# The mLSTM's gates made ahead of its queries, keys and values; the first key lists fetched behind the retention

## What is computed

```
# block 1, after attention and retention
x = x + mix @ w_out
q = (rmsnorm(x) @ w_query)                      # routing of PEER
s = einsum('thpd,hpnd->thpn', q, sub_keys)      # sub_keys: the "key lists"
# block 2, token mixer
c_gate, b_gate, x_in, q, k, v, o, i_pre, f_pre, ga, gm = split(h @ w_in)
ya = b_gate * causal_dwconv(c_gate * x_in)
q, k = split(silu(causal_dwconv(concat(q, k))))
logf = log_sigmoid(f_pre + b_fgate);  b = cumsum(logf)
dlog = b[t] - b[s] + i_pre[s];  m_t = max over s <= t
num = sum_s (q.k) * exp(dlog - m_t) * v;  den = sum_s (q.k) * exp(dlog - m_t)
h = num / max(|den|, exp(-m_t))
```

## Time and profile before

| what | us |
|---|---|
| median of 3 runs (3684.33 to 3688.38) | 3687.12 |
| the profiled execution's own time | 3683.72 |
| span of its trace | 3681.7 |

### The profile page before, as it was taken

The page is one execution under the profiler, slowest core; times in us unless marked ns, Lnnn a source line. Parts: engine busy times, 40 slices in busy tenths (PEclk is TensorE's granted clock), DMA queues, the critical chain, the costliest instruction groups (busy, mean ns, idle before and its releaser), DMA issues.

```text
span 3681.7 us, 48844 instructions
## 1 busy us (share of the span) xinstructions
PE 3364.6 (91%) x16134; PEld 1980.3 (54%) x16134; DVE 2283.8 (62%) x4836; ACT 1237.1 (34%) x3239; POOL 699.0 (19%) x602
## 2 busy tenths in 40 slices
PE   7987899988999999996998999979978999999997
PEld 3444567334666666662443544446654566666664
DVE  1063696877887877773131600049898788877677
ACT  1141112667554552001011110021287655455101
POOL 0000001222333333330000000000042233333332
PEclk9998999999999999997998899989979999999998
DMA  3100225989999999992121012212489899999997
GB/s 144 69 24 23 92 91 205 416 344 354 381 420 416 407 394 417 408 421 91 68 80 52 23 69 80 80 69 91 153 309 354 336 419 405 418 411 393 417 422 310
DMA packets 129928, 927.24 MB, mean 252 GB/s; under 512 B 14800, under 2 KB 15744, under 8 KB 18184
## 3 DMA queue, kind: packets, MB, share of 16 engines
q0 software_dynamic: 73728, 536.90, 35.9%
q1 hardware_dynamic: 52368, 377.51, 26.0%
q10 hardware_dynamic: 3704, 11.36, 0.8%
HBM read 923.59 MB, written 2.12 MB: 251 GB/s over the span
## 4 chain that ended last, share of the span: by engine, by line
PE 57%; DMA 17%; DVE 10%; issue 9%; ACT 5%; DVEq 1%; another core or an unknown queue 1%; POOL 1%; POOLq 0%; SPq 0%; ACTq 0%
PE proj L445 18%; DMA ring<-in_experts,idx 14%; PE proj L437 10%; PE proj L684 9%; PE obk L675 7%; PE proj L584 5%; DVE xn L1425 3%; PE tps L630 2%; ACT hot L970 2%; DVE ring L1408 2%; DMA wring<-in_slabs 2%; PE proj L615 1%; PE tps L410 1%; PE obk L781 1%; ACT hot L974 1%
## 5 line engine op out<-in xcount | busy, mean ns | idle before, releaser
L684 PE MATMUL proj<-wring,hT 128*128 128x512 f32 x2048 | 957.7, 611 | 62.0 <-DVE hT L1464 61.8
L390 POOL DMA_INDIRECT ring<-in_experts,idx x512 | 668.3, 1305 | 1360.8 <-DVE xn L1425 1252.3
L1408 DVE SCALAR_TENSOR_TENSOR ring<-ring,xn 128x1024 f32<-128x1024 f32 x512 | 608.6, 1220 | 179.2 <-DMA ring<-in_experts,idx 178.5
L675 PE MATMUL obk<-hT,wring 128*128 128x256 f32 x3072 | 694.2, 379 | 0.0
L675 PEld LDWEIGHTS obk<-hT,wring 128*128 128x128 f32 x3072 | 583.5, 190 | 159.5 <-issue 87.5
L1425 DVE SCALAR_TENSOR_TENSOR xn<-ring,coef,xn 128x1024 f32<-128x1024 f32 x512 | 628.6, 1280 | 22.5
L684 PEld LDWEIGHTS proj<-wring,hT 128*128 128x128 f32 x2048 | 379.6, 193 | 454.3 <-issue 380.6
L970 ACT ACTIVATE hot<-iotab,away 128x128 bf16<-128x128 bf16 x1856 | 567.2, 391 | 6.6 <-DMA ada_rows<-hT 6.2
L445 PE MATMUL proj<-hT,wring 128*128 128x512 f32 x1280 | 559.3, 596 | 9.2 <-DMA ring<-in_keys 5.2
L445 PEld LDWEIGHTS proj<-hT,wring 128*128 128x128 f32 x1280 | 244.3, 191 | 311.4 <-issue 310.6
L437 PE MATMUL proj<-wring,hT 128*128 128x512 f32 x768 | 330.7, 592 | 4.5 <-ACT hT L848 1.9
(11 more groups left out here) (237 smaller groups left out, 2072.1 us busy)
## 6 DMA issues: line engine op xcount, KB each, us to landing
wring<-in_slabs SPq DMA_DIRECT2D x356, 1024.0 KB
ring<-in_experts,idx POOLq DMA_INDIRECT x512, 9.6
x_res<-in_x SPq DMA_DIRECT2D x1, 2048.0 KB, 9.8
ring<-in_keys ACTq DMA_DIRECT2D x2, 1024.0 KB, 6.8
out<-x_res SPq DMA_DIRECT2D x4, 512.0 KB, 2.6
ring<-ada_rows ACTq DMA_DIRECT2D x1, 1536.0 KB, 6.8
ring<-in_norm_pre ACTq DMA_DIRECT2D x2, 512.0 KB, 7.0
ring<-ada_rows ACTq DMA_DIRECT2D x1, 1024.0 KB, 19.3
```

The lines of the kernel that those rows point to most:

```text
L390: pool.indirect_dma_start(rows[:, r, :], None, d[f"experts{layer + 1}"], bass.IndirectOffsetOnAxis(idx[:, k, r:r + 1], 0)).then_inc(row[r] ...
L675: m = pe.matmul(obk[:, j % 2, 0:DT], wring[:, k, at + c * P:at + (c + 1) * P], hT[:, c, GB * P:T], start=(c == 0), stop=(c == DC - 1))
L684: m = pe.matmul(proj[:, 2 * b + c, :], coef_t[:, j % 2, b * P:(b + 1) * P], wring[:, k, at + c * 512:at + (c + 1) * 512], start=False, sto ...
L1408: v.scalar_tensor_tensor(rows[:, r, 0:D], rows[:, r, 0:D], 1.0, xn[:, r % GB, :], ALU.mult, ALU.mult, accum_out=dots[:, r:r + 1]).then_inc ...
```

## The change

Nothing is computed otherwise; only orders change.

- PE makes the gates' products (L746) right behind the convolution's, ahead of the wait for the convolution's last read; turns the gates' columns (L754) behind the queries and keys; and issues gate_rows(0) and gate_rows(1) behind the values, ahead of the wait that all values were read.
- ACT does abs, exp, ln and exp of the gates ahead of its copies of queries and keys, and copies the columns between the last silu and the first copy of the values.
- DVE does its part of the gates behind the first convolution, ahead of clearing the border of the second.
- ACT asks for the first key lists behind its second square root (L925) instead of at L1079.

```diff
@@ PE @@
             transposed(S_CONV, N_CONV, hT)
-            all_read(S_QK2)
-            transposed(S_QK2, N_QK, hT)
-            all_read(S_V2)
-            token_major(S_V2, N_V, hT)
+
             pe.wait_ge(in_lstm, 16 * 4)
             for g in range(2):
                 ...
             m.then_inc(if_done, 1)
+            all_read(S_QK2)
+            transposed(S_QK2, N_QK, hT)
             pe.wait_ge(rows_ready, 1)
             ...
             t.then_inc(cols_done, 1)
-            pe.wait_ge(cols_ready, 2)
-            all_read(S_O2)
-            pe.wait_ge(qk_ready, 8)
-            pe.wait_ge(v_ones, 1)
             ...
+            all_read(S_V2)
+            token_major(S_V2, N_V, hT)
+            pe.wait_ge(cols_ready, 2)
+            gate_rows(0)
+            gate_rows(1)
+            all_read(S_O2)
+            pe.wait_ge(qk_ready, 8)
+            pe.wait_ge(v_ones, 1)
             for h in range(MH + 1):
                 if h < MH:
-                    gate_rows(h)
+                    if h >= 2:
+                        gate_rows(h)
                     lstm_scores(h)
@@ ACT @@
             root(sv16, sv16, P, hn_done)
+            act.dma_start(subk, d["keys1"]).then_inc(in_keys, 16)
             norm_turned(TR_MIX, hT)
@@
-            act.dma_start(subk, d["keys1"]).then_inc(in_keys, 16)
             route(0, S_WQ1, ACT.Gelu)
@@ ACT, behind the loop of L1098 @@
+            act.wait_ge(if_act, 1)
+            ... Abs, Exp, Ln
+            act.wait_ge(if_act, 2)
+            act.activation(mrow[0:MH, 4, :], mrow[0:MH, 4, :], ACT.Exp, scale=-1.0).then_inc(rows_ready, 1)
             act.wait_ge(mm_free, 4 * S_QK2 + 4)
             ...
             qk_silu(N_QK * 4 - 1)
+            act.wait_ge(cols_done, 1)
+            for g, t in enumerate((acol, ecol)):
+                ...
             for s in range(N_V):
                 ...
-            (the same lines, from if_act to the copies of the columns, taken out here)
             act.dma_start(mhg, d["mh_norm_w_2"]).then_inc(in_mhg, 16)
@@ DVE, behind the loop of L1553 to L1560 @@
+            v.wait_ge(in_lstm, 16 * 4)
+            v.wait_ge(if_done, 1)
+            ... the gates' eleven instructions
             v.wait_ge(mm_free, 4 * S_QK2 + 4)
             v.memset(cx[:, :, 0:3], 0.0).then_inc(qk_conv, 1)
             ...
             v.memset(vaug[:, :, :, P:P + 1], 1.0).then_inc(v_ones, 1)
-            (the same lines taken out here)
```

More of the change, by code:

```diff
@@ L1098, in _ @@
                 act.activation(csb[:, j % 2, :], proj[:, job % 4, :], ACT.Copy).then_inc(c_copied, 1)
+            act.wait_ge(if_act, 1)
+            steps.inc(act.activation(mrow[0:MH, 0, :], mrow[0:MH, 1, :], ACT.Abs))
+            steps.wait()
+            steps.inc(act.activation(mrow[0:MH, 0, :], mrow[0:MH, 0, :], ACT.Exp, scale=-1.0))
+            steps.wait()
+            act.activation(mrow[0:MH, 0, :], mrow[0:MH, 0, :], ACT.Ln, bias=1.0).then_inc(ln_done, 1)
+            act.wait_ge(if_act, 2)
+            act.activation(mrow[0:MH, 4, :], mrow[0:MH, 4, :], ACT.Exp, scale=-1.0).then_inc(rows_ready, 1)
             act.wait_ge(mm_free, 4 * S_QK2 + 4)
@@ L1113, in _ @@
             qk_silu(N_QK * 4 - 1)
+            act.wait_ge(cols_done, 1)
+            for g, t in enumerate((acol, ecol)):
+                act.activation(t, tps[:, g, 0:TB * MH].rearrange("p (b h) -> p b h", b=TB),
+                               ACT.Copy).then_inc(cols_ready, 1)
             for s in range(N_V):
@@ L1118, in _ @@
                                    ACT.Copy).then_inc(mm_free, 1)
[L1121 to L1128, removed]
             act.dma_start(mhg, d["mh_norm_w_2"]).then_inc(in_mhg, 16)
[L1130 to L1133, removed]
             for n in range(MH * TB):
@@ L1560, in _ @@
                 v.tensor_tensor(yaT[:, j, :], ctmp[:, k, :], proj[:, (job + 2) % 4, :], ALU.mult).then_inc(mm_free, 1)
+            v.wait_ge(in_lstm, 16 * 4)
+            v.wait_ge(if_done, 1)
+            g = [mrow[0:MH, k, :] for k in range(5)]
+            v.tensor_scalar(g[2], obk[0:MH, 0, :], bif[:, 0:1], None, ALU.add)
+            link(v.tensor_scalar(g[1], obk[0:MH, 1, :], bif[:, 1:2], None, ALU.add))
+            v.memset(dots[:, :], 0.0).then_inc(if_act, 1)
+            v.wait_ge(ln_done, 1)
+            link(v.scalar_tensor_tensor(g[1], g[1], 0.0, g[0], ALU.min, ALU.subtract))
+            link(v.memset(g[0], 1.0))
+            link(v.tensor_tensor_scan(g[4], g[0], g[1], 0.0, ALU.mult, ALU.add))
+            link(v.tensor_tensor(g[2], g[2], g[4], ALU.subtract))
+            link(v.tensor_tensor_scan(g[3], g[2], g[2], 0.0, ALU.max, ALU.max))
+            link(v.tensor_tensor(g[4], g[4], g[3], ALU.add))
+            v.tensor_scalar(g[3], g[3], -1.0, None, ALU.mult).then_inc(if_act, 1)
             v.wait_ge(mm_free, 4 * S_QK2 + 4)
@@ L1578, in _ @@
             v.memset(vaug[:, :, :, P:P + 1], 1.0).then_inc(v_ones, 1)
[L1582 to L1595, removed]
             def weight_arg(n):
```

## The result

The changed kernel takes 3660.74 us (median of 4 runs, 3658.34 to 3665.19); the kernel before, with one more run beside them, 3686.9 us (4 runs). The ratio is 0.9931, with a 95% interval of 0.9914 to 0.9948: 26 us faster, 19 to 32 by the interval. The forecast was 3663.4, with a range of 3652 to 3676.

A forecast was written before the change was run, and what follows sets the result against it. PE, or the chain through it, was taken to bound the kernel, so reordering pays only where it waits. Key lists 5.9, gates and opening 17.8, rest of loop 0: 23.7 us off 3687.12 gives 3663.4 us, range 3652 to 3676.

The forecast's parts named there:

- The chain behind the key lists: First routing: earlier key lists start PE's queries 4.25 us sooner, plus 1.6 us from the clock; bounds 4.2 and 5.9, 5.9 taken.
- The rival in which the experts' stage takes it back: First routing: the earlier key lists give nothing, leaving 17.8 us alone and 3669 us; chance 0.11.
- The gates up to the values' end: Gates' products go ahead of queries and keys, 13.9 us, saving a 1.06 us wait; values end at E + 12.9.
- E: Origin of the count: the end of the values' products in the kernel before, at 1980.1.
- The cover of the chain: PE fills four banks in 27.6 us while the gates' chain runs; first copy at about 13.2 us, price nothing.
- The columns' transposes: Behind the last tile of queries and keys, where PE waited 0.87 us anyway: 0 to 0.2 us, taken as 0.
- The table load: One more ACT table switch behind the values, 1.28 us; price 0.1 us, or 0.9 us by the Trainium skill's page.
- The opening: Heads' loop start: first quotient 15.2 us (warm) or 18.2 us (cold) behind the values, gaining 20.8 or 17.8 us.
- cold case: Opening at half clock, values(0) 4.67 and gate_rows(2) 2.07 us: first quotient at 18.2 us, gain 17.8 us, taken for the forecast.
- the second place: The gates up to the opening of the heads' loop, where PE was idle 12.62 us for ACT; gain forecast 17.8 us.
- warm bound: Opening at full clock: first quotient 15.2 us behind the values, gain 20.8 us; rival warm throughout had chance 0.12.
- The rest of the loop: As many cold heads as before, 0 us; bounds 6.3 us gained all warm, 14.2 us lost with all six cold.

The follow-up runs named there:

- keys_only: The kernel before with only the first key lists asked for behind the second square root, gates left where they were: 3665.63 against 3672.95 us, ratio 0.9982.
- keys_late_2: The changed kernel with 20 scratch copies on ACT ahead of a late key-list request: queries start 28 us later, key scores to first convolution product 1287.10 us.
- chain_16: The changed kernel with 16 idle fills added to the gates' chain on DVE: queries and keys took 55.20 us as before.
- chain_48: The changed kernel with 48 idle fills added to the gates' chain on DVE: PE waited 16.5 us once, queries and keys took 74.0 us.
- full-depth kernels: The changed kernel with gate rows and scores on 128-partition operands, the additional ones zero, some variants with further edits: loop 44.7 to 45.9 us in four profiles.
- deep_rows: The changed kernel with only the gate rows' operands filled with zeros to 128 partitions: ratio 0.9916 to the kernel before, loop 46.43 us.
- deep_scores: The changed kernel with operands of gate rows and scores filled with zeros to 128 partitions: ratio 0.9916 to the kernel before, loop 45.86 us.

## Why the prediction was right, step by step

- **The chain behind the key lists** The earlier trace rows passed the gain on whole: 4.05 us up to the queries and 1.63 for the clock, against 4.25 and 1.6. The choice between the bounds, by the second block's start, was right, 0.97 and 14.00 to the digit. The rival in which the experts' stage takes it back falls by `keys_only` and `keys_late_2`.
- **The gates up to the values' end**: E + 12.6 against E + 12.9. The cover of the chain was right in mechanism and size: first copy ended 13.1 us behind PE's start, and `chain_16` and `chain_48` show both ends of it. The columns' transposes cost 0.94 us with their wait, where the wait was 0.87.
- **The table load** cost nothing: it started at 1986.86 and ACT's next exp at 1988.16, 1.30 us later. The exp came 0.79 us behind the start of DVE's argument, as before (1987.37 to 1988.16; 2010.20 to 2010.99). The drain of the Trainium skill's page ("ScalarE: Activation LUTs", section "What ACT_TABLE_LOAD costs") would have held that exp for 1.4 us more; it is not in this row, and the 0.9 us by that page did not appear.
- **The opening**: 16.37 us from the values to the first quotient, between the bounds of 15.2 and 18.2 but outside the 17 to 19 that I named as the sign to look for. The mis-sized term is the cold case: I made values(0) and gate_rows(2) cold throughout (4.67 and 2.07 us), but the clock was up again before values(0) ended, so they took 4.11 and 1.12. That is 1.5 us; the first weighted score came 0.4 later than my 3.1. This term makes most of the difference between the 17.8 us forecast for the second place and the 20.0 measured. The full-depth kernels came at 13.8 to 14.05, below my warm bound by 1.2 or more: that bound was too high. In the 10.07 us that I read as work "without a pause" DVE had waited 1.05 us for a gate row at half clock, and I carried this wait over into the warm case:

```profile
2016.69 0.75 DVE L1603 TENSOR_SCALAR ring<-tps,stat 128x512 f32<-128x512 f32 x1 [1.05 <-PE tps L764]
```

- **The rest of the loop** as cold as before: 52.55 against 52.69 us. An agreement within 0.2 us was luck: in the other kernels with the same operands the loop took 49.5 to 56.1. But one to three gaps of 9.5 us or more came in each, never six, and the changed kernel's second profile had the same gaps as its first, so it was less open than the 14.2 us I allowed for. The other bound, 6.3 us for an all-warm loop, left out the first gap before (7.83 us, also above 6.72): the full-depth loops were 6.8 to 8.0 us shorter than before.
- **Sum**: 5.7 + 20.0 in the profiles against 5.9 + 17.8, with 0.75 us gained ahead of the first place, 0.17 in the stage between and 1.5 lost behind O, the last two in stages that vary by more than that. So the forecast was right for its reasons in the waits and hops, and some 2 us short by the opening. The rule of the Trainium skill's page "TensorE: Matmul & The Clock Gate", section "What's actually happening", that activity releases the throttle, would have made the opening warm; the window from 1988.00 to 1995.40, busy for all of its 7.40 us at 0.54, disagrees, and the full-depth kernels show what it leaves open: here it mattered which operands the busy engine had.

## What to carry to other kernels

A chain of small operations between two engines costs its length only where the dense engine waits for it; move its head in front of a dense stretch, and compare its length with what the dense engine can do before it lacks a buffer (here four banks, 27.7 us). A transfer asked for at the moment of need costs its own latency (here 4.1 us) and then, on TensorE, the clock that falls meanwhile (here 1.6 us); look for the same code elsewhere in the trace without the wait, since it prices both. A clock gained in one stage may be lost in the next (here 8.9 us gained, 4.0 lost again in one profile): judge it by the whole kernel, not by the stage.

## What the runs showed of the hardware

The depth of the operands, with columns unchanged, decided the granted clock in the heads' loop: with 64-partition scores and 8-partition rows it fell to 0.50 in nine of nine profiles, also with PE busy for 15.85 of 16 us; with 128-partition ones, filled up with zeros, it stayed at 1.00 up to the last head's scores in four of four, with PE busy for 31.2 of 39 us. Full-depth rows with 64-partition scores (`deep_rows`, one profile) came close to the latter, 46.43 us for the loop, with a clock of 0.96 where `deep_scores` had 1.00. Filling up with zeros cost no time on PE: 3.5 us in the changed kernel and 3.4 in `deep_scores` from a head's gate row to the end of its scores, both at full clock. And a wait of DVE for its own previous instruction added 0.16 us behind a fill of 0.48, 0.645 us in all.
